# A mixture-of-experts stage in two classes of experts, 128-row blocks and 64-row blocks

## The reference

```python
logits = (t @ w_router) + b_router
vals, idx = lax.top_k(logits, TOP_K)              # 4 of 32
gates = jax.nn.softmax(vals, axis=-1)
...
u = jnp.einsum('nrd,ndf->nrf', xs, w_up[block_e]) + b_up[block_e][:, None, :]     # 1024 -> 512
glu = jnp.minimum(u[..., ::2], SWIGLU_LIMIT)
lin = jnp.clip(u[..., 1::2], -SWIGLU_LIMIT, SWIGLU_LIMIT)
a = glu * jax.nn.sigmoid(SWIGLU_ALPHA * glu) * (lin + 1.0)                        # 256 wide
y = jnp.einsum('nrf,nfd->nrd', a, w_down[block_e]) + b_down[block_e][:, None, :]  # 256 -> 1024
```

## Time and profile before

| | us |
|---|---|
| median of 3 runs | 1534.92 (1533.69 to 1536.91) |
| span of the profiled execution | 1535.06 |
| TensorE busy in it | 1303.3 |
| VectorE, ScalarE, GpSimd busy | 637.4, 248.4, 489.0 |
| DMA, mean over the span | 221 GB/s |

### The profile page before, as it was taken

The page is one execution under the profiler, slowest core; times in us unless marked ns, Lnnn a source line. Parts: engine busy times, 40 slices in busy tenths (PEclk is TensorE's granted clock), DMA queues, the critical chain, the costliest instruction groups (busy, mean ns, idle before and its releaser), DMA issues.

```text
span 1535.1 us, 17763 instructions
## 1 busy us (share of the span) xinstructions
PE 1303.3 (85%) x4216; PEld 666.8 (43%) x4217; DVE 637.4 (42%) x1538; ACT 248.4 (16%) x565; POOL 489.0 (32%) x667
## 2 busy tenths in 40 slices
PE   7886688899889899986996887499989899888965
PEld 3545344444444444434544445244444444444422
DVE  0667125555555222259546766322222222122216
ACT  0111111111111111121113432111111111111111
POOL 0016533334443333323100025333333333333313
PEclk9987699999999999998996998599999999999987
DMA  9963579997897555562135504255746577566434
GB/s 359 360 246 137 223 266 351 350 355 282 313 344 277 218 191 207 181 230 104 61 137 193 196 1 189 77 200 196 266 181 234 211 296 270 191 250 258 158 117 164
DMA packets 92244, 339.22 MB, mean 221 GB/s; under 512 B 17321, under 2 KB 39593, under 8 KB 74674
## 3 DMA queue, kind: packets, MB, share of 16 engines
q1 hardware_dynamic: 50098, 284.23, 49.3%
q0 software_dynamic: 21312, 33.61, 6.0%
q10 hardware_dynamic: 20800, 20.97, 4.0%
HBM read 338.55 MB, written 44.04 MB: 249 GB/s over the span
## 4 chain that ended last, share of the span: by engine, by line
PE 64%; DVE 10%; issue 8%; POOL 5%; DMA 4%; SPq 4%; POOLq 2%; ACT 2%; DVEq 0%; ACTq 0%
PE ps L821 25%; PE ps L834 16%; PE ps L807 5%; POOL onehot L622 4%; PE ps L996 4%; PE ps L1054 2%; DMA ring<-in_w_ada 2%; PE ps L713 2%; PE ps L890 2%; DMA big<-y_rows 2%; SPq L382 1%; SPq L385 1%; PE ps L796 1%; PE ps L753 1%; DVE big L1342 1%
## 5 line engine op out<-in xcount | busy, mean ns | idle before, releaser
L821 PE MATMUL ps<-ring,work 128*128 x576 | 260.4, 606 | 34.8 <-SPq L427 33.6
L821 PE MATMUL ps<-ring,big 128*128 x576 | 255.7, 597 | 33.8 <-SPq L427 33.6
L834 PE MATMUL ps<-ring,work 128*128 x576 | 261.6, 597 | 2.0 <-ACT work L1143 2.0
L1478 DVE TENSOR_SCALAR work<-ps 128x256 f32<-128x256 f32 x72 | 30.6, 425 | 482.0 <-PE ps L821 482.0
L622 POOL TENSOR_SCALAR onehot<-cst,rank_now 128x128 bf16<-128x128 f32 x312 | 183.9, 602 | 16.4 <-POOL rank_now L616 16.4
L821 PEld LDWEIGHTS ps<-ring,work 128*128 128x128 f32 x576 | 108.9, 193 | 169.7 <-issue 169.3
L821 PEld LDWEIGHTS ps<-ring,big 128*128 128x128 f32 x576 | 107.2, 190 | 164.9 <-issue 164.5
L643 POOL COPY scatter_at<-scatter_ring 128x1 int32 (+1 forms) x72 | 14.1, 196 | 494.3 <-DVE work L1497 252.6
L834 PEld LDWEIGHTS ps<-ring,work 128*128 128x128 f32 x576 | 103.8, 190 | 107.0 <-issue 105.6
L1139 ACT ACTIVATE work<-work 128x256 f32<-128x256 f32 x72 | 30.0, 417 | 578.9 <-DVE work L1478 578.9
L713 PE MATMUL ps<-ring,c_sig 128*128 128x512 f32 x160 | 75.8, 634 | 16.1 <-DMA ring<-in_w_ada 15.3
(11 more groups left out here) (202 smaller groups left out, 1665.8 us busy)
## 6 DMA issues: line engine op xcount, KB each, us to landing
ring<-in_w_up SPq DMA_DIRECT2D x64, 2048.0 KB, 7.9
ring<-in_w_down SPq DMA_DIRECT2D x64, 1024.0 KB, 10.9
ring<-in_w_ada SPq DMA_DIRECT2D x18, 2048.0 KB, 14.5
big<-y_rows SPq DMA_DIRECT2D x8, 2048.0 KB, 7.9
big<-in_w_ada ACTq DMA_DIRECT2D x12, 1024.0 KB, 10.4
big<-in_w_kv_ada ACTq DMA_DIRECT2D x8, 1024.0 KB, 11.6
h_rows<-big SPq DMA_DIRECT2D x8, 512.0 KB, 6.9
ring<-in_w_q SPq DMA_DIRECT2D x2, 2048.0 KB, 10.6
```

What stands on the lines that cost most here:

```text
L821: mm = pe.matmul(U, xT[p][:, k, :], ring[:, bass.ds(at + k * UP, UP)], start=False, stop=(k == KC - 1))
L834: mm = pe.matmul(Y[:, h, :], aT[:, k, :], ring[:, bass.ds(at + k * D + h * HALF, HALF)], start=(k == 0), stop=(k == KF - 1))
```

## The change

The 32 experts of a layer are sorted into two classes as the kernel runs. Those with more than 64 rows are large; if they are fewer than sixteen, experts with fewer rows join them in order of their number; if they are more, all 32 become large and the static blocks are empty. The large ones come first, in 128-row blocks and the loop of before (now six peeled blocks). Then sixteen small blocks follow, unrolled, one for each small expert, of 64 rows. In these, the up and down projections are made of two column tiles: the 64 rows stand twice in the array, and the first half of the output columns goes to partitions 0 to 63, the second to 64 to 127. Gathers and scatters of a small block move half rows, 2 KB for each of 128 partitions. Its engines do the same steps with half the columns; y is copied by VectorE alone.

The weights are loaded in the order of the classes (T_LOAD), so all loads of a stage now follow the table; up weights in runs of 8 KB, down weights of 4 KB instead of 16 and 8. The up projection waits for the up weights alone and the down projection for the others, and SyncE passes on the weights two experts ahead. The first three small blocks are prepared (`pick_small`) on GpSimd after blocks 1, 3 and 5. Routing gets more VectorE steps, 41 where 14 were between the rank and the columns, and five row matmuls instead of two. `dynamic_dma_scratch_size` is 8192. Ten of the twenty pieces of layer 0 fall into small blocks.

```diff
-PEELED = 4
+PEELED = 6
+NSMALL = 16
+NLARGE = NE - NSMALL
+ROWS2 = 64
...
+        xT2 = [xT[1][:, 4 * j:4 * j + 4, :].rearrange("p c t -> p (c t)") for j in range(2)]
+        y_sb2 = [y_sb[0][:, j * HALF:(j + 1) * HALF] for j in range(2)]
...
-            def load_expert(l, e, r):
+            def load_expert(l, q, r):
+                e = sp.value_load(table[0:1, bass.ds(q + T_LOAD, 1)], min_val=0, max_val=NE - 1)
...
+                sp.wait_ge(s["table_ready"], l + 1)
+                for r in range(RING):
+                    wait_free(n0 + r)
+                    load_expert(l, r, r)
                 pass_on(0, 0)
+                pass_on(1, 0)
                 meanwhile()
-
-                sp.wait_ge(s["table_ready"], l + 1)
                 with sp.Fori(0, NE // RING - 1) as turn:
                     for r in range(RING):
 
-                        pass_on((r + 1) % RING, turn + (r + 1) // RING)
-                        e = turn * RING + r
-                        end = sp.value_load(table[0:1, bass.ds(e + T_END, 1)], min_val=1, max_val=48)
+                        pass_on((r + 2) % RING, turn + (r + 2) // RING)
+                        q = turn * RING + r
+                        end = sp.value_load(table[0:1, bass.ds(q + T_END, 1)], min_val=1, max_val=64)
                         sp.wait_ge(m[l]["down_done"], end)
-                        load_expert(l, e + RING, r)
+                        load_expert(l, q + RING, r)
...
-            for e in (1, 2, 0, 3):
-                wait_free(expert_start[1] + e)
-                load_expert(1, e, e)
...
+                def pick_small(t):
+
+                    e = pool.value_load(table[0:1, T_LOAD + NLARGE + t:T_LOAD + NLARGE + t + 1], min_val=0, max_val=NE - 1)
+                    n = pool.value_load(table[0:1, T_BASE2:T_BASE2 + 1], min_val=0, max_val=TILES)
+                    if t:
+                        pool.wait_ge(q["place_mm2"], z + t)
+                    pool.tensor_tensor(rank_now2[:, :], rank[:, :, bass.ds(e, 1)].rearrange("p i o -> p (i o)"),
+                                       cst[:, bass.ds(n + C_BLOCK, 1)].to_broadcast([P, TILES]), ALU.subtract
+                                       ).then_inc(q["select_step2"], 1)
+                    pool.tensor_copy(sel2[:, t % RING:t % RING + 1], bf_sel[:, bass.ds(e, 1)]).then_inc(q["select_step2"], 1)
+                    pool.wait_ge(q["select_step2"], 3 * (z + t) + 2)
+                    for i in range(TILES):
+                        ins = pool.tensor_scalar(onehot2[:, i, :], cst[:, C_SLOT2:C_SLOT2 + P], rank_now2[:, i:i + 1], None,
+                                                 ALU.is_equal)
+                    ins.then_inc(q["select_step2"], 1)
+
+                def gather_small(t):
+                    if t >= 2:
+                        pool.wait_ge(q["xg_turned2"], z + t - 1)
...
+                def scatter_small(t):
+                    pool.wait_ge(q["y_ready2"], z + t + 1)
+                    pool.wait_ge(q["row_step2"], 3 * (z + t) + 3)
...
                 for b in range(PEELED):
                     body(b, b % 2)
...
+                    if b % 2:
+                        pick_small(b // 2)
+                    if b >= 3 and b % 2:
+                        gather_small(b // 2 - 1)
...
                 scatter(last, 1, last_pair=pair)
+                for t in range(NSMALL):
+                    if t + 2 < NSMALL:
+                        gather_small(t + 2)
+                    if t + 3 < NSMALL:
+                        pick_small(t + 3)
+                    if t:
+                        scatter_small(t - 1)
+                scatter_small(NSMALL - 1)
...
+                def up_small(t):
+                    u = ps[0][:, t % 2, 0:FF]
+                    at = t % RING * SLOT
...
+                    for j, half in enumerate(halves2):
+                        pe.matmul(u[half, :], sel2[:, t % RING:t % RING + 1].to_broadcast([3 * NE, ROWS2]),
+                                  bup3[:, j * FF:(j + 1) * FF], start=True, stop=False)
+                    pe.wait_ge(q["up_weights_landed"], NLARGE + t + 1)
+                    pe.wait_ge(q["xT_ready2"], z + t + 1)
+                    for k in range(KC):
+                        rows = xT2[t % 2][:, k % 4 * P + k // 4 * ROWS2:k % 4 * P + (k // 4 + 1) * ROWS2]
+                        for j, half in enumerate(halves2):
+                            mm = pe.matmul(u[half, :], rows, ring[:, at + k * UP + j * FF:at + k * UP + (j + 1) * FF],
+                                           start=False, stop=(k == KC - 1))
+                    mm.then_inc(q["up_done2"], 1)
...
+                for t in range(NSMALL):
+                    up_small(t)
+                    if t + 3 < NSMALL:
+                        places_small(t + 3)
+                    if t + 1 < NSMALL:
+                        turn_small(t + 1)
+                    if t == 0:
+                        pe.wait_ge(q["y_act"], last + 1)
+                        pe.wait_ge(q["y_dve"], last + 1)
+                    else:
+                        down_small(t - 1)
+                    turn_a_small(t)
+                down_small(NSMALL - 1)
...
+                for t in range(NSMALL):
+                    clamp_small(t)
+                    if t + 3 < NSMALL:
+                        rows_small(t + 3)
+                    finish_small(t)
+                    if t:
+                        copy_y_small(t - 1)
+                    j = t + NLARGE - 2 - PEELED
+                    if l == 0 and j < PIECES:
+                        piece(j, j % 2)
+                copy_y_small(NSMALL - 1)
...
-    nc = bacc.Bacc("TRN2", target_bir_lowering=False, num_devices=1)
+    nc = bacc.Bacc("TRN2", target_bir_lowering=False, num_devices=1, dynamic_dma_scratch_size=8192)
```

More of the change, by code:

```diff
@@ L492, in _ @@
                 load_static(k)
[L493 to L497 removed]
+            store_h(0)
             sp.wait_ge(s["gcol_ready"], 1)
@@ L852, in body, with places_small @@
                     turn_a(b)
+                def places_small(t, last=None):
+                    e = pe.value_load(table[0:1, T_LOAD + NLARGE + t:T_LOAD + NLARGE + t + 1], min_val=0, max_val=NE - 1)
+                    pe.wait_ge(q["select_step2"], 3 * (z + t) + 3)
+                    if last is not None:
+                        pe.wait_ge(q["row_step"], last * 2 + 7)
+                    if t:
+                        pe.wait_ge(q["row_step2"], 3 * (z + t) - 2)
+                    for i in range(TILES):
+                        mm = pe.matmul(J2(t), onehot2[:, i, :], vals[:, i, bass.ds(e, 1), :].rearrange("p a v -> p (a v)"),
+                                       start=(i == 0), stop=(i == TILES - 1))
+                    mm.then_inc(q["place_mm2"], 1)
@@ new lines, in down_small @@
+                def down_small(t):
+                    y = ps[1][:, t % 2, :]
+                    at = t % RING * SLOT + KC * UP
+                    pe.wait_ge(q["weights_landed"], NLARGE + t + 1)
+                    pe.wait_ge(q["aT_ready2"], z + t + 1)
+                    if t >= 2:
+                        pe.wait_ge(q["y_ready2"], z + t - 1)
+                    for k in range(KF):
+                        for j, half in enumerate(halves2):
+                            mm = pe.matmul(y[half, :], aT2[:, k * ROWS2:(k + 1) * ROWS2],
+                                           ring[:, at + k * D + j * HALF:at + k * D + (j + 1) * HALF],
+                                           start=(k == 0), stop=(k == KF - 1))
+                    mm.then_inc(q["down_done2"], 1)
@@ L1429, in route @@
-                link(dve.tensor_scalar(last, ends[0:1, NE - 1:NE], -1.0, None, ALU.add))
-                link(dve.tensor_scalar(last, last, 1, None, ALU.bitwise_or))
-                link(dve.tensor_scalar(table[0:1, T_PAIR:T_PAIR + 1], last, 1, None, ALU.logical_shift_right))
-                link(dve.tensor_scalar(table[0:1, T_END + NE - 1:T_END + NE], last, 1.0, None, ALU.add))
+                count, ends, large, order, place, other, until, seen = (blocks[:, j, :] for j in range(8))
+                flag, limit, edge, total, turned, room = (class_col[:, j:j + 1] for j in range(6))
@@ new lines, in route @@
+                part, part1 = cst[:, C_PART:C_PART + 1], cst[:, C_PART1:C_PART1 + 1]
+                ones = bf_ones[:, 0:NE]
+                step(dve.tensor_scalar(count, totals, float(P), 1.0, ALU.is_gt, ALU.add))
+                link(dve.tensor_scalar(large, totals, float(ROWS2), None, ALU.is_gt))
+                step(dve.scalar_tensor_tensor(out=count, in0=totals, scalar=float(2 * P), in1=count,
+                                              op0=ALU.is_gt, op1=ALU.add))
+                link(dve.tensor_tensor_scan(order, ones, large, 0.0, ALU.mult, ALU.add))
@@ new lines, in route @@
+                link(dve.scalar_tensor_tensor(out=large, in0=order, scalar=limit, in1=large, op0=ALU.is_le, op1=ALU.max))
```

(20 more changed lines are left out.)

355 lines of the change are left out of this document (240 added, 115 removed).

## The result

The changed kernel took 1499.43 us (median of 4 runs, 1497.11 to 1500.9) against 1535.59 (4 runs, 1533.69 to 1536.91) of the kernel before beside it: ratio 0.9767 [0.9752, 0.9782]. It is 36 us faster, where 64 was forecast. The time lies outside the 1445 to 1495 that the forecast gave itself, and inside the 1495 to 1512 of rival (b).

A forecast was written before the change was run, and what follows sets the result against it. TensorE's nearly unbroken work with GpSimd's one-hot close behind and SyncE's weight waits bound the kernel. Per layer 446.6 + 7 against 484.96 and 486.09 took 63.9 off 1535.06: forecast 1471, range 1445 to 1495 (8 in 10: 1432 to 1512).

The forecast's parts named there:

- rival (b): Small blocks: late gather or y buffer, or 0.8 us mode changes; period 12.3 us, total 1495 to 1512; chance 0.14.
- Part 1: Block counts per layer: 20 large and 16 small blocks, where 36 large ones ran.
- Part 2: Large blocks: 13.07 us periods set by GpSimd's one-hot, 11.6 us for three small-block preparations; stage 277.2 us.
- TensorE's own 12.7: Large blocks: TensorE's own work put at 12.7 us a block, against 13.07 with GpSimd's one-hot late.
- Part 3: Small block on TensorE: column tiles side by side, up 3.5, down 1.85, whole block 6.9 us, no mode-change charge.
- Rival (d): Small blocks: column tiles don't overlap; up +3.4, down +1.75, period 12.3 us, total 1532; chance 0.06.
- Part 4: Small blocks: GpSimd loop sets the period, 10.3 us, 11.2 with half clock for a third of TensorE's work; phase 169.4.
- Rival (c): Small blocks: TensorE stays at half clock through the phase; period 13.3 us, total 1562; chance 0.09.
- Part 5: Weight transfers: best DMA rate 366 GB/s, 9.4 us a small expert; price 0, up to 10 us.
- rival (a): Small blocks: GpSimd loop doesn't bind and DMA does; total 1431; chance 0.12.
- Part 6: Stage start: longer routing 3.0 and 0.5, first gather under load 3.4 more; together 7 us a layer (3 to 12).

The follow-up runs named there:

- experiments four and five: On the changed kernel, four: small blocks' up projection computed twice, 1487.58 us; five: small blocks' tile 0 matmuls all ordered before tile 1's, 1483.45 us.
- experiment seven: Only the weights passed on two experts ahead, on the kernel before: 1523.39 us, ratio 0.9927.
- experiment three: Changed kernel with GpSimd's one-hots of both large and small blocks made one block earlier: 1363.56 us, ratio 0.8877.

## Why the prediction was right and wrong

The direction and the mechanism of the small blocks held. The size was forecast nearly twice as large, and the sum missed by 24 us. The time falls where rival (b) had it, but not for its reasons: TensorE waited 0.7 us in all for a gather in the small blocks of layer 1 and not at all in those of layer 0, never for a y buffer, and no gap shows where the tiling mode changes. The small blocks of layer 0 came near its period of 12.3 us because the clock was lower than forecast (experiments four and five), so it is luck that its range has the result.

**Part 1** held: 20 large and 16 small blocks a layer.

**Part 2** named the right queue and missed the sizes. The stage took 285.4 us for 277.2. (i) The last twelve full periods of layer 0 took 161.5 us, 13.46 each for 13.07, together 4.7 us more. Where VectorE has a piece, in the first seven of them, they were 13.58, with GpSimd's transfers longer, which experiment seven shows without any class; I took a block of the earlier trace rows that has none and applied it to all. The five without a piece, such as 427.80 to 441.13 in the chain, were still 13.2 and 13.4 by turns, with 1.15 and 1.34 us instead of 1.05 from the start of turn_rows to down; what lengthens the turn wasn't found. (ii) From the first up projection to the eighth, which starts at 283.05, 105.5 us passed, 13.8 more than 7 periods of 13.1, where the three preparations were put with 11.6. Of the 8.2 us some 1.3 aren't placed. The largest error in the reading of the kernel was one that the sum didn't show: "TensorE's own 12.7". It made the one-hot's wait look like 0.4 us a block, and so I never looked for the time that lay in the order of the queue. It is 1.1 us a block; with the preparations, which then fit in the slack, 74 us in all.

**Part 3** held: up 3.62 for 3.5, down 1.94 for 1.85 at full clock, a whole block 6.59 for 6.9. The Trainium skill (TensorEngine Tiling, Key Properties) has it that a mode change drains TensorE. The runs show a block with its changes 0.3 us shorter than the sum that had no charge for them, which leaves no room for the 0.8 us of rival (b). Rival (d) is excluded by up itself, 3.62 us side by side and 6.26 in sequence.

**Part 4** had the loop right to its last step and the clock too mild. The first small down ended 18.9 us after the last large one (18.7). Then eleven periods took 136.3 us in layer 0 and 127.1 in layer 1 against 123.2, and the rest 23.6 and 23.5 against 27.5. That layer 1's phase (168.4) met the forecast (169.4) is luck: two errors of 4 us cancel. I had the clock low for a third of the loop's TensorE work. In layer 0 it was low for the whole of down in six of the eleven (3.68 us) and for part of it in the others (2.85 to 3.24): 2.1 us a block on the 10.7 of experiment four make 12.8, and most blocks were 12.1 to 12.9. The 10.7 themselves are 0.4 over layer 1's 10.3, where VectorE has no pieces. Places, put as doubling, took 0.56, and 0.55 at full clock in experiment four. So the mechanism stood, the weight of its two ends didn't; experiments four and five show it from both sides. Rival (c) didn't come: TensorE got its clock back by each block's up projection, or within it (3.62 us in most blocks, 3.7 to 4.1 in the others).

**Part 5** was right for a wrong reason. 366 GB/s of the earlier trace rows was no ceiling: from 976 to 978 us of the changed kernel,

```profile
976.00:978.00 2.00, 0.42 (x4) 0.29 (x3) 0.47 (x3) 0.00 (x0) 0.97 (x1) 0.50 1.05 434
```

As long as the blocks came every 12 us no small up waited for weights. In experiment three, at 386 GB/s through the whole phase, layer 0 is held by the pieces, through their bytes or through VectorE's wait for them. Something like rival (a) thus comes after the queue is mended, not instead of it; how much of it is the transfers isn't shown.

**Part 6** was short. Layer 0 started 5.3 us later; between the stages 11.0 were lost for the 7 put. TensorE's wait for the block columns (waits of the whole run), the first gather of layer 1 (timeline: its issue, and the turn that needs it) and its first up weights (chain) were

```profile
PE ps L846 <- DVEq L1645: 14.3, 2, 7.2
```

```profile
971.08 1.13 POOL L651 DMA_INDIRECT work<-h_rows,gather_at  x1 [0.16 <-issue]
...
980.00 1.98 PE L882 MATMUL ps<-cst,work 128*128 128x128 f32 x8 [3.59 <-DMA work<-h_rows,gather_at]
...
983.03 1.22 PE L898 MATMUL ps<-ring,work 128*128 x1 [0.61 <-SPq L457]
```

```profile
966.93 16.03 DMA ring<-in_w_up
```

7.2 us a layer where it was 3.2 before: +4.0, put with 3.5. The gather landed 8.9 us after issue, put with 8.6, and from the transposes of the gates (L854) to the first up it grew by 3.7. The weights, put as landing ahead of the gather, landed 3 us behind it, 16.0 us after issue for the 7.7 put. The first up waits for them last, although the copied rows came no earlier than 982.71: two paths end together there, and one of them wasn't in the sum. The rest wasn't in it either, or was put smaller: the last scatter of layer 0 landed after 5.34 us instead of 3.44, the row matmuls to the gates' transposes took 3.87 instead of 3.16, and some 0.7 us aren't placed. That layer 0 lost only 5.3 in spite of these has to do with an opening that ran 3.2 us earlier; that expert weights are no longer loaded behind the conditioning weights is my reason for it, and it is argued, not shown.

**In all:** large stages +8.2 and +6.9, small phases +9.4 and -1.0, starts and seams -1.7 and +4.0, tail -1.8: 24 us, the distance from 1471 to the span of 1495.2.

## What to carry to other kernels

In a queue that runs in order, put the step whose inputs are there early ahead of the one that waits for the end of the loop: here that was worth 136 us of 1499, and it decided whether the smaller blocks were worth 24 us or some 80. Take a short idle time that recurs in every block, with one releaser, as the sign of a loop and not as its price; follow the loop once round and ask which of its members needn't be in it. And when an engine that isn't the bound is made faster, look at its granted clock behind the new gap, since steps of it that do lie in the loop pay for it.

## What the hardware showed unexpectedly

- More work on TensorE made the kernel faster: 12 us with the up projections doubled, 16 us with their two tiles in sequence. With an idle gap of 2.6 to 4.0 us in every block of some 12 the granted clock was 0.82 and 0.86 on average in the two small phases, and turn and down behind the gap ran wholly or in part at the lower level in nearly every block; with gaps near 1 us it was 0.99, with none 1.00.
- A wait for another engine, 0.4 us on record in front of four small matmuls, cost 1.1 us a block.
- Two column tiles with four matmul records each ran side by side even when all of one stood ahead of the other in the program; with sixteen each, only four of them did.
- GpSimd's indirect transfers took 1.26 to 1.28 us to issue a gather in blocks in which VectorE multiplied a piece, 1.01 to 1.03 in the others; that the one causes the other isn't shown.
- One core moved 434 GB/s for 2 us and 386 for 160 us; in that stretch three pieces of 1 MB on ScalarE's queue took 23 to 29 us to land, 11.1 in the median of the changed kernel.
